# Feed-forward input projection: block products that add onto seeded accumulators

## What is computed

```python
h = rms_norm(x, ffn_pre_gain[l])                  # 256 x 2048
gt, up = jnp.split(h @ w_ffn_in[l], 2, axis=-1)   # 2048 x (5632 + 5632)
x = x + rms_norm((jax.nn.silu(gt) * up) @ w_ffn_out[l], ffn_post_gain[l])
```

## Time and profile before

| | |
|---|---|
| three runs | 1494.03 us (median), 1493.93 to 1494.49 |
| span of the profiled execution | 1491.6 us, so 2.4 us of the median lie around it |
| TensorE busy | 1481.7 us, 99% of the span |
| DVE busy, ACT busy | 1137.2 us (76%), 835.4 us (56%) |
| granted TensorE clock, mean | 0.999 |
| the ten bodies (831.7 to 1253.3 us) | 421.6 us |

### The profile page before, as it was taken

The page is one execution under the profiler, slowest core; times in us unless marked ns, Lnnn a source line. Parts: engine busy times, 40 slices in busy tenths (PEclk is TensorE's granted clock), DMA queues, the critical chain, the costliest instruction groups (busy, mean ns, idle before and its releaser), DMA issues.

```text
span 1491.6 us, 19212 instructions
## 1 busy us (share of the span) xinstructions
PE 1481.7 (99%) x6712; PEld 1220.6 (82%) x6712; DVE 1137.2 (76%) x1353; ACT 835.4 (56%) x1018; POOL 151.4 (10%) x286
## 2 busy tenths in 40 slices
PE   9999999999999999999999999999999999999997
PEld 7888887888888888888888888888888888888886
DVE  6878988855554577657576788888888888887897
ACT  6645455565666544656678455555555555555554
POOL 0000000140220000000000221012222221100000
PEclk9999999999999999999999999999999999999999
DMA  9755555565555655856463666766666667656564
GB/s 342 235 186 178 182 180 186 189 208 187 188 192 171 239 183 185 334 195 211 161 197 116 198 209 221 230 212 216 209 212 199 198 217 236 231 173 213 187 208 169
DMA packets 89859, 305.08 MB, mean 205 GB/s; under 512 B 13056, under 2 KB 13568, under 8 KB 88768
## 3 DMA queue, kind: packets, MB, share of 16 engines
q1 hardware_dynamic: 80144, 285.12, 57.6%
q0 software_dynamic: 9216, 18.63, 3.9%
q10 hardware_dynamic: 432, 0.45, 0.1%
HBM read 294.19 MB, written 2.10 MB: 199 GB/s over the span
## 4 chain that ended last, share of the span: by engine, by line
PE 99%; DMA 0%; DVE 0%; SPq 0%; ACT 0%; issue 0%; DVEq 0%
PE acc L1808 10%; PE acc L1809 10%; PE acc L1810 10%; PE acc L2128 5%; PE acc L2131 5%; PE acc L2130 5%; PE side L2130 5%; PE side L2131 5%; PE side L2128 5%; PE side L1808 4%; PE side L1809 4%; PE side L1810 4%; PE tr L1808 3%; PE tr L1809 3%; PE tr L1810 3%; PE side L2093 2%
## 5 line engine op out<-in xcount | busy, mean ns | idle before, releaser
L548 ACT ACTIVATE w_hi<-raw 128x1024 fp32r<-128x1024 f32 x299 | 315.1, 1060 | 295.4 <-PE acc L2131 90.2
L1001 DVE TENSOR_TENSOR w_lo<-raw,w_hi 128x1024 fp32r<-128x1024 f32 x262 | 320.9, 1227 | 202.0 <-ACT w_hi L529 197.7
L1006 DVE TENSOR_TENSOR w_lo<-raw,w_hi 128x1024 fp32r<-128x1024 f32 x315 | 381.5, 1222 | 102.8 <-ACT w_hi L548 92.9
L529 ACT ACTIVATE w_hi<-raw 128x1024 fp32r<-128x1024 f32 x262 | 276.9, 1059 | 281.3 <-PE acc L1810 165.6
L1808 PE MATMUL acc<-w_hi,xT_hi 128*128 128x512 f32 x504 | 198.3, 393 | 0.5 <-DVE w_lo L1001 0.5
L1810 PE MATMUL acc<-w_hi,xT_lo 128*128 128x512 f32 x504 | 196.3, 389 | 0.0
L1809 PE MATMUL acc<-w_lo,xT_hi 128*128 128x512 f32 x504 | 196.3, 389 | 0.0
L503 POOL DMA_DIRECT2D hT_st<-h_blk x176 | 93.6, 540 | 492.1 <-DVE h_blk L1073 453.6
L1808 PEld LDWEIGHTS acc<-w_hi,xT_hi 128*128 128x128 f32 x504 | 94.6, 188 | 22.6 <-issue 2.6
L1810 PEld LDWEIGHTS acc<-w_hi,xT_lo 128*128 128x128 f32 x504 | 94.6, 188 | 20.0
L1809 PEld LDWEIGHTS acc<-w_lo,xT_hi 128*128 128x128 f32 x504 | 94.7, 188 | 18.9
(11 more groups left out here) (468 smaller groups left out, 2747.3 us busy)
## 6 DMA issues: line engine op xcount, KB each, us to landing
raw<-in_units SPq DMA_DIRECT2D x530, 512.0 KB, 3.9
hT_st<-h_blk POOLq DMA_DIRECT2D x176, 32.0 KB, 1.8
x_tok<-in_x SPq DMA_DIRECT2D x4, 512.0 KB, 5.9
qkT<-qk_blk POOLq DMA_DIRECT2D x64, 32.0 KB, 2.9
xres<-in_x POOLq DMA_DIRECT2D x1, 2048.0 KB, 11.0
m_raw<-in_mem_t POOLq DMA_DIRECT2D x1, 2048.0 KB, 8.6
mq<-in_mem POOLq DMA_DIRECT2D x1, 2048.0 KB, 15.4
x_raw<-in_x_t SPq DMA_DIRECT2D x6, 256.0 KB, 6.4
```

Of the source, the lines that this page charges most:

```text
L529: a_.activation(w_hi[:, j % RING], raw[:, j % RING], ACT.Copy).then_inc(hi_ready, 1)
L548: a_.activation(w_hi[:, v % RING], raw[:, slots[block]], ACT.Copy).then_inc(hi_ready, 1)
L1001: v_.tensor_tensor(w_lo[:, s], raw[:, s], w_hi[:, s].bitcast(F32), ALU.subtract).then_inc(lo_ready, 1)
L1006: v_.tensor_tensor(lo[:, v % RING], raw[:, slot], hi[:, v % RING].bitcast(F32), ALU.subtract).then_inc(lo_ready, 1)
```

## The change

The work of TensorE stays the same in count: seven block products for one k group in each pair 1 to 10, and plain units for the rest. New is where the products stand and where they land.

**Banks.** The gate chunk of body i owns two banks (`acc` and `tr` in turn), the up chunk two others (`side[0:2]` and `side[2:4]` in turn). Block products add onto these. Where the scheme needs a partial sum in two places, the bank is *seeded*: after the first product ACT copies gate bank 0 to up bank 1 (`u2_seeded`, L1041); after the second ACT copies gate bank 1 to SBUF (`e_sb`, L1046); DVE writes up bank 0 as up bank 1 + `e_sb` (`up0_seeded`, L1758); ACT copies up bank 1 to gate bank 1 (`gate1_seeded`, L1050); DVE adds `e_sb` onto up bank 1 (`up1_seeded`, L1761). The adds of before (L1642 to L1674) are gone; silu (L1030) reads the gate banks, the product with up (L1725) the up banks.

**Order.** Three of the up units of body i-1 are set among the block products of body i. A body i of 2 to 10 now is, with step numbers from 0:

| step | what | matmuls | waits for, beside its split |
|---|---|---|---|
| 0 | product B11 into gate bank 0 | 6 | silu of body i-2 |
| 1 | up unit of body i-1 | 12 | `up1_seeded` of body i-1 |
| 2 | product T1 into gate bank 1 | 6 | |
| 3 | product B21 into gate bank 0 | 6 | `u2_seeded` |
| 4 | product T2 onto up bank 1 | 6 | |
| 5 | up unit | 12 | |
| 6 | product T3 onto up bank 1 | 6 | `up0_seeded` |
| 7 | product B22 onto up bank 0 | 6 | |
| 8 | up unit | 12 | |
| 9 | product T4 onto gate bank 1 | 6 | `gate1_seeded` |
| 10-12 | three up units of body i-1 | 36 | |
| 13-18 | six gate units of body i | 72 | |

Body 1 has one more difference: only four up units of chunk 0 are left for it, so it has 17 steps. It begins at step S_FI, which is 280 now (284 before); the last six up units follow body 10. S_FO, where the second feed-forward product begins, is 474 in both.

**Raw slots.** `late_raw` has four more weight buffers, usable up to body 10, and `late_units()` gives every load the slot that is free first. The two further slots in the code are for more than one k group and are not used (`PAIRS` is 1 everywhere).

```diff
+PAIRS = (0, 1, 1, 1, 1, 1, 1, 1, 1, 1, 1)
+EARLY_SLOTS, GROUP_SLOTS = 4, 2 if max(PAIRS) > 1 else 0
...
+        t1 = [total(k[g][B11], k[g][B12], k[g][B11], now()) for g in range(b.p)]
+        step(rest[0], 0, t1)
...
+        t3 = [total(k[g][B12], k[g][B22], k[g][B12], 0) for g in range(b.p)]
+        step(rest[1], 0, t3)
+        t4 = [total(k[g][B11], k[g][B21], k[g][B11], b.p6) for g in range(b.p)]
+        for g in range(b.p):
+            step(k[g][B12], t3[g][4], t4 if g == 0 else ())
...
+            for b in BODIES:
+                i = b.i
+                for v in range(b.first, b.end):
+                    if v == b.first and i > 1:
+                        gate_silu(i - 1)
+                    if v == b.p1 - 1:
+                        act.wait_ge(unit_used, b.p1)
+                        if i > 1:
+                            act.wait_ge(up_taken, 2 * i - 2)
+                        a_.activation(up_bank(i, 1), gate_bank(i, 0), ACT.Copy).then_inc(u2_seeded, 1)
+                    if v == b.p5 - 1:
+                        act.wait_ge(unit_used, b.p5)
+                        if i > 1:
+                            act.wait_ge(up1_seeded, i - 1)
+                        a_.activation(e_sb[:], gate_bank(i, 1), ACT.Copy).then_inc(p5_copied, 1)
...
+                    split_late(v + RING)
...
-            def gate_sum(i, h):
-
-                dve.wait_ge(unit_used, body_base(i) + 12 + h)
-                if h == 1:
-                    dve.wait_ge(u_done, i)
-                v_.tensor_tensor(silu_g[:, h], acc[:, h], silu_g[:, h], ALU.add).then_inc(acc_taken[h], 1)
...
+            for b in BODIES:
+                i = b.i
+                for v in range(b.first, b.end):
+                    if v == b.p6 - 1:
+                        dve.wait_ge(unit_used, b.p6)
+                        dve.wait_ge(p5_copied, i)
+                        v_.tensor_tensor(up_bank(i, 0), up_bank(i, 1), e_sb[:], ALU.add).then_inc(up0_seeded, 1)
+                    if v == b.p7 + 1:
+                        dve.wait_ge(gate1_seeded, i)
+                        v_.tensor_tensor(up_bank(i, 1), up_bank(i, 1), e_sb[:], ALU.add).then_inc(up1_seeded, 1)
...
+                    split_late(v + RING)
...
+                pe.wait_ge(up0_seeded, i)
+                for g in range(b.p):
+                    late_product(v + g, ups[1], *sum_of(S_hi[g], S_lo[g], 2), False)
```

More of the change, by code:

```diff
@@ L60 @@
 G_S5, G_PRE, G_PROJ, G_MID, G_GLU, G_GATE, G_BR, G_OUT, G_MK, G_XQ, G_MV, G_XO, G_FI, G_FO = (
-    0, 1, 4, 12, 13, 15, 23, 35, 39, 40, 41, 42, 46, 68)
+    0, 1, 4, 12, 13, 15, 23, 35, 39, 40, 41, 42, 46, 47)
 T_GLU, T_BR, T_X1 = 0, 2, 10
-FI_SPLITS, FO_SPLITS, FO_LAST = 19, 53, 56
-S_FI, S_FO, S_END = 284, 474, 583
-def late_units():
[L69 to L80, removed]
-        for _ in range(count):
[L82 to L100, removed]
@@ L101, in late_units @@
     for count in (12, 8, 4):
-        plain(count)
-        pair()
-    plain(8)
+        out_plain(count)
+        out_pair()
+    out_plain(8)
     for count in (4, 8, 4, 4):
[L106 to L119, removed]
+        out_plain(count)
+        out_pair()
+    out_plain(8)
+    first, last = {}, {}
@@ new lines, in late_units @@
+    for n, (key, _, sums) in enumerate(steps):
+        for k in [key] + [k for t in sums for k in t[:3]]:
+            first.setdefault(k, S_FI + n)
+            last[k] = S_FI + n
+    free = [S_FI - RING + 1 + k for k in range(RING)] + [0] * (SLOTS - RING)
+    rounds = [S_FI // RING] * RING + [0] * (SLOTS - RING)
+    loads, place = [], {}
+    for key in sorted(first, key=lambda k: first[k]):
+        slots = list(range(RING))
+        if last[key] < bodies[9].blocks:
+            slots += range(RING, RING + EARLY_SLOTS)
+        if bodies[1].first <= first[key] and last[key] < bodies[7].blocks:
+            slots += range(RING + EARLY_SLOTS, SLOTS)
+        slot = min(slots, key=lambda k: free[k])
+        assert free[slot] <= first[key]
+        rounds[slot] += 1
+        place[key] = slot, rounds[slot] * 16
+        loads.append((key, slot, free[slot]))
+        free[slot] = last[key] + 1
@@ L122 @@
+    plan = {}
+    for n, (key, t, sums) in enumerate(steps):
+        plan[S_FI + n] = place[key] + (t, [tuple(place[k] for k in a[:3]) + a[3:] for a in sums])
+    return loads, plan, bodies, s_fo, now()
+LATE_LOADS, LATE_STEPS, BODIES, S_FO, S_END = late_units()
 N_X, N_GM, N_Y1, N_MEM, N_X1, N_Y2, N_X2, N_Y3 = range(8)
@@ L949, in _ @@
+            for v in range(BODIES[9].end, S_FO):
+                if v == BODIES[9].end:
+                    gate_silu(10)
+                split_late(v + RING)
             preload(3, ACT.Sqrt)
@@ L2234 @@
             k0, k1 = 2 * plain[2 * g], 2 * plain[2 * g + 1]
-            order += [left[k0:k1], right[k0:k1]] + blocks_of(left, right, g)
-        order += [left[2 * end:], right[2 * end:]]
+            outs += [left[k0:k1], right[k0:k1]] + blocks_of(left, right, g)
+        outs += [left[2 * end:], right[2 * end:]]
+    for n, block in enumerate(_np.concatenate(outs)):
+        late["out", n] = block[None]
+    order += [late[key] for key, slot, splits in LATE_LOADS]
     def turned(a):
```

401 lines of the change are left out of this document (253 added, 148 removed).

## The result

| | before | after |
|---|---|---|
| median of the runs timed together | 1494.17 us (1493.93 to 1494.49, 4 runs) | 1506.06 us (1505.53 to 1506.19, 4 runs) |
| ratio, 95% interval | | 1.0078 [1.0064, 1.0093] |
| span of the profiled execution | 1491.6 us | 1504.1 us |
| granted clock, mean | 0.999 | 0.999 |

What follows compares the result with a forecast made beforehand. TensorE, without a gap in the ten bodies, was taken to bound the kernel. Late seeds add 7.4 us in bodies 2 to 10, late steps 1.9 in body 1: 1494.03 + 9.3 = 1503.3 us, range 1495.8 to 1509.5.

Steps and rivals of the forecast that it cites:

- The frame: In the ten bodies TensorE has no gap: DVE's saved work gains nothing, each new wait not met adds its whole length.
- rival (b): Ten bodies: faster, by a matmul pace under 0.227 us; 1% of 421.6 us would give 1489.8; chance 0.04.
- the four buffers: Weight buffers: can end ACT's waits for transfers, 27.6 us in 35 cases, but TensorE waited for none; worth nothing.
- rival (a): Bodies 2 to 10: the seed of up bank 0 is in time, nothing lost there; 1494 to 1497 us; chance 0.15.
- (c): Seeds in the bodies: PSUM writes are dear, or one body's delay doesn't drain; 1509 us, over 1507; chance 0.10.
- the mechanism: Step 6 of each body: the seed of up bank 0 queues on DVE behind splits and differences, so TensorE waits.
- seed starts after step 0: Steady body: DVE starts the seed of up bank 0 at 10.80 us after step 0, ending at 11.48.
- step 6 late, bodies 2 to 10: TensorE goes on at 11.70 instead of 10.88 us of the body: 0.82 late, nine times, 7.4 us.
- body 1, step 5 and step 6 late: Body 1, no silu but a late lead-in: step 5 late by 0.63, step 6 by 1.28, together 1.9 us.
- lead-in and bodies together: The sum of the losses: 7.4 us in bodies 2 to 10 and 1.9 in body 1, 9.3 us.
- rival (d): Seeds in the bodies: waits exist but shorter, by cheap restart and cheap writes; 1499.5 us, low end of the main case.
- The rest equal: Outside the ten bodies and ten us before them, nothing changes; that stretch itself gets 9 us longer.

Runs made afterwards that it cites:

- the two changes of order: Two runs, each against the changed kernel: seed of up bank 0 one split sooner on DVE, 1496.96 us; silus nine steps later on ACT, 1499.01 us.

## Why the prediction was right

**The frame held.** TensorE had no slack to give, and no kernel here beat before: rival (b) has nothing for it. What DVE was relieved of, 37 us, was worth nothing, as said. So were the four buffers: with them ACT's splits in the bodies (L641) wait for no transfer at all, where the 27.6 us before all lay in the bodies, and TensorE has nothing of that.

The measured 1506.06 lies in the stated range, but the range took in other stories too: half of rival (a) and half of (c). What bears the mechanism out are the ten waits at the line that was named, their size, and the two changes of order that took most of them away.

**Point by point**, predicted and measured, in us:

| step | predicted | measured |
|---|---|---|
| copy L1041, seed L1758 | 0.58, 0.68 | 0.58 to 0.60, 0.69 |
| seed starts after step 0 | 10.80 | 10.79 |
| step 6 late, bodies 2 to 10 | 0.82 each | 0.77 at the wait, 0.80 by the length of a body |
| body 1, step 5 and step 6 late | 0.63 and 1.28 | 0.67 and 1.28 |
| lead-in and bodies together | 9.3 | 9.26 |
| the rest of the program | 0 | 2.6 of run time (11.9 - 9.3) |

Body 1 by its own rows, DVE and then TensorE of after:

```profile
824.12 1.22 DVE L1121 TENSOR_TENSOR w_lo<-raw,w_hi 128x1024 fp32r<-128x1024 f32 x1
825.54 1.23 DVE L1139 TENSOR_TENSOR raw<-raw,raw 128x1024 f32<-128x1024 f32 x1 [0.20 <-DVE w_lo L1121]
...
834.72 0.69 DVE L1758 TENSOR_TENSOR side<-side,e_sb 128x512 f32<-128x512 f32 x1
```
```profile
831.45 0.50 PE L2222 MATMUL side<-w_hi,xT_hi 128*128 128x512 f32 x1 [0.40 <-DVE w_lo L1121]
...
834.07 0.39 PE L2224 MATMUL side<-w_hi,xT_lo 128*128 128x512 f32 x1
835.46 0.50 PE L2209 MATMUL side<-w_hi,S_hi 128*128 128x512 f32 x1 [1.00 <-DVE side L1758]
835.80 0.40 PE L2210 MATMUL side<-w_lo,S_hi 128*128 128x512 f32 x1
```

The second matmul, 835.80, comes 1.73 after 834.07 where the pace makes 0.45: 1.28 late. Step 5 by the same count, from 830.66 to 831.78, is 0.67 late. In the steady bodies no difference stands directly behind the split that it waits for in the stretch that counts, so the dearer waits cost nothing there: with two waits instead of four the lead-in and the bodies take 452.66 us, against 452.62. In body 1 the forecast was a little low: two differences there start 1.36 and 1.42 us behind their splits, not 1.26. The seed comes 12.14 us after the start of step 280 (822.58), where 11.89 were reckoned.

**Why rival (a) fell.** It needed the seed 0.8 us sooner. Moving the seed up by one split, 1.13 us, is just that, and it took the waits of bodies 2 to 10 away: the rival was right on what it would be worth and wrong on the order. That its 1496 and the 1496.96 of that kernel are close is in part luck: the rival's 2 us are body 1, where the trace has 0.9, and the second product, of which it said nothing, has 2.5 more. Rival (c) fell by the measured lengths of L1041 and L1758. Of rival (d)'s 0.38 us a body 0.02 to 0.05 came.

**Where it was off.** "The rest equal" was wrong by 2.6 us of the median. I gave the differences before and after the same price of 1.26 us and looked at the second product not at all, since no line of it seemed to change; yet the helper that feeds it did (`split_late`, with its list of waits), and so did its table of slots. The second product is 1.5 to 1.7 us longer in both profiles of after; the experiments don't show which of the two it is, or whether it is either. The other part lies ahead of step 276: 1.54 us in the profile of after, 0.41 in its second profile (step 276 at 810.57, the stretch behind it again 452.65 long), so most of it is scatter of an execution. It is a first split later by 0.54 us (the matmul at 13.38 instead of 12.84), 0.2 at 701 us and 0.75 at 784. In the nine other profiles of changed kernels step 276 starts at 809.96 to 811.00, in the three of before and before with more waits at 810.15 to 810.18. By the same count the second profile, with a span of 1502.8, has 9.3 + 0.4 + 1.5 = 11.2 us over before.

## What to carry to other kernels

Where TensorE has no idle time, reckon a change by the queue ahead of each new operation that TensorE waits for: add the pitches from the last point where that engine was idle. Here 1.13 us of place in the queue was worth 8.2 us in ten bodies, and 37 us less work nothing. And look at every stretch that a changed helper feeds: one that no line of the change speaks of was 1.5 us longer here, for a cause that stays open.

## What the runs showed of the hardware

- ACT and DVE write PSUM at the price of SBUF: the copy from PSUM to PSUM took 0.58 to 0.60 us (to SBUF 0.60), the sum from PSUM to PSUM 0.69, against 0.68 to SBUF and 0.69 within SBUF. On DVE the Trainium skill, Perfetto Trace Analysis, section Optimizing Scalar/DVE Operations, gives an overhead of about 60 ns an instruction on SBUF and 125 on PSUM; these rows don't show the difference.
- Waits that are met long since aren't always free. A DVE operation with up to four semaphores to wait for, behind the split that it needs, started 1.42 us after that split; with two, the halves first, 1.25 to 1.26; with two, the transfer first, 1.32. The same in two kernels, after and before with more waits. A difference that doesn't need the split just ahead of it started 1.13 to 1.15 us behind it in after, with three or four semaphores in its list.
- An operation on DVE that isn't waited for cost nothing ten times over (1505.71 against 1505.38 and 1506.06), while the same in the queue ahead of the seed cost 0.57 to 0.60 each.
- Idle time of TensorE can cost its clock. With two groups in some pairs the granted clock fell to 0.52 to 0.55 five times, once after 4.8 us of idle time, four times after 1.4 and 2.5 us, and matmuls started 0.43 us apart instead of 0.227. In after, with 0.5 to 1.0 us of wait a body, it was 1.00 over the bodies.
